# Selective scan issued between the tiles of the z, q, k and v projection, and two empty pieces of the expert loop left out

## The reference, cut to what matters

```
z, xbc, dt_f, dt_b, q, k, v, pin, gates = split(h @ w_in)          # h: modulated RMSNorm of x
ssd:   xbc = silu(conv5(xbc) + b);  xs (16 heads x 64), B, C (4 groups x 64)
       a = softplus(dt + bias) * -exp(a_log);  cs = cumsum(a) in each chunk of 128 tokens
       y[l] = sum_{s<=l} (C_l . B_s) exp(cs_l - cs_s) dt_s x_s  +  exp(cs_l) C_l . state      (forward and backward)
       y = rms_norm((y_f + y_b + d_skip * xs) * silu(z))
attn:  q, k normed, rotary on latent tokens, softmax over latent keys and cached context keys
pool:  windows 2, 4, 8, 16
merged = sum_i sigmoid(gate_i) * (branch_i @ w_i_out);  x += g1 * (merged @ w_out)
moe:   16 experts in 4 groups, the best group per token, top 2 in it:  x += g2 * moe(h2)
```

## Time and profile before

| what | value |
|---|---|
| median of the runs | 2563.08 us |
| profiled execution, its own time | 2565.21 us |
| its span on the core | 2563.4 us |
| PE busy, PE weight loads busy | 2225.8 us, 1924.2 us |
| DVE busy, ACT busy | 1517.6 us, 1128.6 us |
| mean granted clock | 0.936 |

### The profile page before, as it was taken

How to read it: one execution, slowest core, us unless ns; L and a number is a source line. 1 busy time by engine, 2 the same in 40 slices (tenths; PEclk the granted TensorE clock), 3 DMA queues, 4 the chain that set the end, 5 groups by cost and what they waited for, 6 DMA issues and landing times. The chain is left out here.

```text
span 2563.4 us, 29114 instructions
## 1 busy us (share of the span) xinstructions
PE 2225.8 (87%) x11340; PEld 1924.2 (75%) x11340; DVE 1517.6 (59%) x2064; ACT 1128.6 (44%) x1453; POOL 8.3 (0%) x12
## 2 busy tenths in 40 slices
PE   5859954599999999999799988993899999999993
PEld 3559943497777789999689988882877777777772
DVE  4857446522655444444454454544587978889784
ACT  4833322223244443333233343332366757667661
POOL 0000000000000000000000000000000000000000
PEclk9979976699999999999899999996899999999995
DMA  6924412144343345554245555640288989889881
GB/s 229 382 69 132 132 54 73 41 125 136 112 130 117 111 136 181 181 181 156 95 149 184 185 164 189 205 157 19 68 283 315 328 276 343 283 302 336 280 287 52
DMA packets 126856, 459.94 MB, mean 179 GB/s; under 512 B 15408, under 2 KB 17232, under 8 KB 126320
## 3 DMA queue, kind: packets, MB, share of 16 engines
q1 hardware_dynamic: 126704, 457.92, 53.1%
HBM read 453.88 MB, written 3.98 MB: 179 GB/s over the span
## 5 line engine op out<-in xcount | busy, mean ns | idle before, releaser
L159 DVE TENSOR_TENSOR wlo<-raw,whi 128x1024 fp32r<-128x1024 f32 x832 | 1005.9, 1223 | 761.5 <-ACT whi L153 748.8
L153 ACT ACTIVATE whi<-raw 128x1024 fp32r<-128x1024 f32 x832 | 870.7, 1058 | 845.5 <-PE bank L171 565.8
L169 PE MATMUL bank<-hhi,whi 128*128 128x384 f32 x1664 | 563.3, 339 | 44.0 <-PEq L891 17.5
L171 PE MATMUL bank<-hhi,wlo 128*128 128x384 f32 x1664 | 558.9, 336 | 0.0
L170 PE MATMUL bank<-hlo,whi 128*128 128x384 f32 x1664 | 558.3, 336 | 0.0
L169 PEld LDWEIGHTS bank<-hhi,whi 128*128 128x128 f32 x1664 | 314.4, 189 | 59.6 <-issue 38.6
L170 PEld LDWEIGHTS bank<-hlo,whi 128*128 128x128 f32 x1664 | 314.2, 189 | 1.6
L171 PEld LDWEIGHTS bank<-hhi,wlo 128*128 128x128 f32 x1664 | 313.9, 189 | 0.0
L1938 PE MATMUL bank<-whi,group_hi 128*128 128x512 f32 x512 | 203.3, 397 | 4.2 <-DVE wlo L159 3.1
L1940 PE MATMUL bank<-wlo,group_hi 128*128 128x512 f32 x512 | 201.2, 393 | 0.0
L1939 PE MATMUL bank<-whi,group_lo 128*128 128x512 f32 x512 | 200.5, 392 | 0.0
(11 more groups left out here) (322 smaller groups left out, 2501.5 us busy)
## 6 DMA issues: line engine op xcount, KB each, us to landing
raw<-in_dense SPq DMA_DIRECT2D x448, 512.0 KB, 3.7
raw<-in_moe SPq DMA_DIRECT2D x384, 512.0 KB, 4.9
cs_rows_bc<-cs_rows SPq DMA_DIRECT2D x8, 768.0 KB, 4.0
x_mix<-in_x SPq DMA_DIRECT2D x1, 3072.0 KB, 14.7
merged<-in_x SPq DMA_DIRECT2D x4, 768.0 KB, 6.7
out_y<-merged SPq DMA_DIRECT2D x4, 768.0 KB, 3.3
pool_w_sb<-in_pool_w SPq DMA_DIRECT2D x1, 1024.0 KB, 6.2
w_router_sb<-in_w_router SPq DMA_DIRECT2D x1, 1024.0 KB, 4.8
```

The costliest lines, as they stand in the source:

```text
L153: self.nc.scalar.activation(self.whi[:, n % W, :], self.raw[:, n % R, :], ACT.Copy).then_inc(self.hi_done, 1)
L159: self.nc.vector.tensor_tensor(self.wlo[:, n % W, :], self.raw[:, n % R, :], self.whi[:, n % W, :].bitcast(F32), ALU.subtract).then_inc(se ...
L169: self.nc.tensor.matmul(out, self.whi[:, s, c], xhi[:, k, :], start=(k == 0), stop=False)
L171: last = self.nc.tensor.matmul(out, self.wlo[:, s, c], xhi[:, k, :], start=False, stop=(k == blocks - 1))
```

## The change

- `ssd_in_phase` keeps only its 24 xbc tiles and now ends with the release of its semaphores and a barrier.
- `ssd_scan_phase`, `ada_settle_phase` and `attn_in_phase` go. In their place `z_qkv_phase` runs the 16 z tiles and the 24 q, k, v tiles as 40 slots, and a `Scan(Side)` object gives each engine a piece of the scan after each slot. Step n takes two slots: slot 11 + 2n (call it A) and slot 12 + 2n (call it B).
- In a step the two DVE instructions L853 and L856 become 12 ACT instructions of 128 x 128: Relu(cs_token - cs_row), with the token's value as the bias, followed by exp with scale -1.
- x is no longer kept by token: each step transposes its own 6 blocks on PE (`turn`), and DVE makes x*dt straight from PSUM in two instructions.
- The conditioning operands are placed at the top of SBUF from the start.
- In the experts, group 0 issues no scatter and the last group no gather; the semaphore counts follow.

```diff
-            N.tile0 += 24
-            N.sp_tiles(sp, 4, 4)
...
-def ssd_scan_phase(N):
...
+class Scan(Side):
+    FIRST, TAIL = 11, 28
...
+    def sp(self, sp):
...
+        for n, (g, d) in enumerate(self.steps):
+            if n >= 2:
+                for _ in range(2 if n > 2 else self.FIRST + 5 - 11):
+                    yield
+                sp.wait_ge(self.s_y, n - 1)
+            sp.dma_start(self.csb[:, n % 2]..., io.scratch[r0:r0 + 4, :]...).then_inc(self.s_csb[n % 2], 16)
...
+    def pe(self, pe):
...
+        for n, (g, d) in enumerate(self.steps):
+            pe.wait_ge(self.s_xdd, n + 1)
+            pe.wait_ge(self.s_stout, n)
+            ...                                        # states, two matmuls
+            yield
+            if n + 1 < len(self.steps):
+                turn(n + 1)                            # 6 transposes, and C.B where a group begins
+            pe.wait_ge(self.s_gated, 2 * g)
+            pe.wait_ge(self.s_m, n + 1)
+            ...                                        # outputs, 12 + 8 matmuls
+            last.then_inc(self.s_y, 1)
+            yield
...
+    def act(self, act):
...
+            act.wait_ge(self.s_csb[n % 2], 16 * (n // 2 + 1))
+            if n >= 2:
+                act.wait_ge(self.s_y, n - 1)
+            A(ec[rows, :, :], csb[rows, n % 2, :, T_CTX:T], ACT.Exp).then_inc(self.s_ec, 1)
+            act.wait_ge(self.s_wsub, n + 1)
+            A(self.wt[:, :, :], self.wt[:, :, :], ACT.Exp).then_inc(self.s_wexp, 1)
+            act.wait_ge(self.s_ec, n + 1)
+            for h in range(4):
+                for c in range(NCH):
+                    hc = 16 * d + 4 * g + h
+                    A(row[:, h, c * P:(c + 1) * P], row[:, h, c * P:(c + 1) * P], ACT.Relu, bias=cstok[:, c, hc:hc + 1],
+                      scale=-1.0).then_inc(self.s_d, 1)
+            act.wait_ge(self.s_d, 12 * (n + 1))
+            A(row, row, ACT.Exp, scale=-1.0).then_inc(self.s_dexp, 1)
+            yield
+            states(n)
+            yield
...
+def z_qkv_phase(N):
...
+            for s in range(slots):
+                if s % 2 == 0:
+                    pe.wait_ge(N.evac, N.blk0 + s // 2 + 1)
+                N.pe_tile(pe, 0, 0, s, N.bank[s // 2 % 2][:, 0:T], N.hhi, N.hlo, 8 * (s % 2), KB)
+                next(beside, None)
...
-def attn_in_phase(N):
...
-                            if t == SCATTER_AT[m]:
+                            if t == SCATTER_AT[m] and i + half:
                                 scatter(i, half, m)
...
+                            if i * 2 + half == NG - 1:
+                                break
                             if t == tiles[0]:
                                 pe.wait_ge(E.s_gl, picked(i, half) + p)
```

More of the change, by code:

```diff
@@ L187, in ada_phase @@
     csilu = N.keep("cond_silu", [P, KB, 2], F32)
[L188 to L193, removed]
+    cst = N.cst = N.keep_top("cond_parts", [P, KB, P], F32R)
+    bada = N.b_ada = N.keep_top("b_ada_sb", [P, 96], F32)
+    rows = N.ada_rows = N.keep_top("ada_rows", [P, 512], F32)
+    four = N.ada_four = N.keep_top("ada_four", [P, 4, 4], F32)
     sq = N.keep("x_squares", [P, 2, 4, T], F32)
@@ L884, in ada_settle_phase @@
[L884 to L898 removed]
+    N.tile0 += 24
@@ L1095, in __init__ @@
         self.sq = keep("head_squares", [P, 2, T], F32)
-        N.at = at = max(N.at, end)
+        N.at = max(N.at, end)
+        self.vt = keep("v_tok", [P, 4, 256], F32)
+        S["gate_at"], N.at = N.at, N.arena
+        at = N.at
         self.sel = keep("head_sel", [P, 10, 32], F32)
@@ L1806, in group @@
                             N.act_hi(act, i, body, half * GL + t)
-                        if t < 4:
+                        if t < 4 and i + half:
                             out_high(i, half, t)
@@ L1817, in group @@
                         for p, (bank, _tiles, at) in enumerate(PICKS):
-                            if t == at:
+                            if t == at and i * 2 + half < NG - 1:
                                 group_high(picked(i, half), p, bank, E.xhi[1 - half])
@@ L1956, in group @@
                             if t == ACT_TR[jj]:
-                                pe.wait_ge(E.s_x, scattered(i, half) * 2 + (2 * sum(at < t for at in SCATTER_AT) + 2))
+                                pe.wait_ge(E.s_x, scattered(i, half) * 2 + (2 * sum(at < t for at in SCATTER_AT if i + half) + 2))
                                 pe.wait_ge(E.s_act, i * 8 + ((g0 + half) * 4 + jj + 2))
@@ L1969, in group @@
                                 last.then_inc(E.s_ga, 1)
-                        if u == 0 and j > 0 and kind != "down":
+                        if u == 0 and j > 0 and kind != "down" and i * 2 + half < NG - 1:
                             pe.wait_ge(E.s_gl, picked(i, half) + sum(at < t for _b, _t, at in PICKS))
```

780 lines of the change are left out of this document (400 added, 380 removed).

## The result

| | before | changed |
|---|---|---|
| median of the runs | 2563.4 us (2561.8 to 2567.1, 4 runs) | 2429.8 us (2429.4 to 2431.3, 4 runs) |
| ratio, 95% interval | | 0.9478 (0.9461 to 0.9494) |
| profiled execution, own time / span | 2565.2 / 2563.4 us | 2430.0 / 2428.2 us |
| mean granted clock | 0.936 | 0.962 |

What follows compares the result with a forecast made beforehand. PE was taken as the bound, idle mainly in the scan; the woven phase, 240.7 us against 333.1, gives 92 us and the experts 21, so 113 off 2565.2 is 2452, less 2.1 for the median: 2450 us, range 2434 to 2485.

Steps and rivals of the forecast that it cites:

- step 3: Woven phase: the scan's own work on PE at full clock, 53.2 us together, of which outputs 26.2 and squares 6.
- step 6: Woven phase: PE's waits inside the scan, 6 us in all (chain for dt 2, first step 2.7, last 0.7); from above 22.
- the experts: Expert groups: first group without scatters, last without gathers; paces give 23 us less, taken as 21, bounds 6 and 28.
- convolution's tail and barrier (1): Before the first z tile: PE idle 7.1 us, 5.4 for the convolution's tail and 1.7 for the phase's end.
- tiles, clock, exit (2, 5): Woven phase: 40 tiles at 4.16 us, 166.4 us, plus 3.7 us for lowered clock and block exit.
- step 5: Woven phase's start and end: lowered clock after PE's idle time, with the block's exit, 3.7 us; from below 0.8.
- step 4: Woven phase: changing over between tile and scan on PE, 0.11 us a slot, 4.3 us for 40; bounds nothing and 13.
- U + 14.8: Scan step opening a group: U ends the tile before slot A; DVE's masked product comes 14.8 us later, PE needs it at 14.9.
- case C: Whole kernel: more gain, with no wait, changeover near zero and 28 us in the experts; 2434 us, chance 0.08.
- A: Scan step: bound by its engine-to-engine chain, 3 us longer, 24 us in all, 2474 us; chance 0.22, alone or with part of B.
- B: Experts: they stay bound by the DMA stream, so only some 7 us come back, 2464 us; chance 0.13.
- D: Woven phase: waits between tiles drop PE's clock to half, making the kernel slower than before, 2674 us; chance 0.03.

Runs made afterwards that it cites:

- the repeat: The changed kernel run once more with nothing altered, beside other kernels: 2429.9 us against 2560.8 for the kernel before, ratio 0.9493.
- experiment 5: Changed kernel with the decay differences moved back from ScalarE to VectorE (subtraction there, twelve Relu gone): 2436.7 us, ratio 0.9519.

## Why the prediction was right in kind and too small

The mechanisms held: the woven phase is PE's own work with few waits, and the experts follow their paces. What failed are three sizes, all on the cautious side: the outputs in step 3 (26.2 for 22.2 us), the waits in step 6 (6 for 2.8), and the experts (21 for 25 us of gain). A further 4 to 7 us came in code that no step names.

The forecast's sum for the woven phase, term by term, with what the traces and the run of the tiles alone gave:

| term (step) | forecast | measured |
|---|---|---|
| convolution's tail and barrier (1) | 7.1 | 6.5 |
| tiles, clock, exit (2, 5) | 166.4 + 3.7 | 169.2 |
| scan on PE, changeovers, waits (3, 4, 6) | 53.2 + 4.3 + 6 | 55.2 |
| sum | 240.7 | 230.9 |

1. *The tail and the barrier* were right: 6.5 us of idle time.
2. *Tiles* and *the clock* (step 5) were right: the clock read 0.93 over the first 23 us behind that idle time, and of the 3.7 us 2.8 were spent.
3. *The scan's own work* (step 3) has the term that failed most. The outputs: 2.14 + 1.14 us a step, 26.2 in all. From 342.59, where the first step's begin, to the next tile at 345.36 it is 2.77 us, 22.2 in all, 4.1 less. I had called the row of 2.14 us in the earlier trace rows one of full clock; a window over just that row reads 0.79, and the same twelve matmuls take 1.77 to 1.80 at 1.00. The squares took 5.3 for 6.
4. *Waits inside* (step 6): 2.8 for 6. The first step's 2.07 (forecast 2.7) and the last one's 0.74 (0.7) were as counted; the chain for dt cost nothing here and 0.2 in the repeat, where I had 2.
5. *Changeovers* (step 4). Outputs, squares and waits make 8.0 of the 63.5 - 55.2 = 8.3 us, so what is left of steps 3 and 4, 4.3 us of changeovers and the small pieces, was right together to 0.3 us. Each by itself wasn't measured, so errors in them may cancel.
6. *The step.* The chain that I followed gave the masked product at U + 14.8 against PE's 14.9. That count was for a step that opens a group, and the trace has it so: 0.15 to 0.3 us ahead in the three such steps behind the first. For the others I had 0.7 us or more, and they have 0.5 to 1.1. The loads on ScalarE and VectorE show the same two kinds of step from the other side. The wait for `cs_rows_bc` never showed, though the rows now take 6.0 us to land instead of 4.0.
7. *The experts.* Group 0: 8.2 for 9, the last group 17 for 14 (142.7 to 142.9 against 159.3 to 160.4 in four executions), 25 in all. The paces alone gave 23; I took off 2 for the stream, and that was wrong: at a DMA share of 0.94 and 0.95 the shortened stretches ran at 1.57 and 1.40 us a tile, under my 1.66 and 1.45.

Together: 102 and 25 make 127 us. The medians fell by 131 and 134 us in the two comparisons; the missing 4 to 7 are no step of mine. The traces have 3.5 and 6.0 us less in code that no edit touches, which is within the spread of one program there; how much of it the change itself gives is not shown. The range was too narrow for two reasons: its lower end was case C's sum (by its own terms 2450 - 6 - 4.3 - 7, so 2433 and not 2434) with nothing left for the error of the other terms, and nothing stood for an execution's draw, some 7 us wide (1171.4 to 1178.1) in the unchanged stretch alone.

The rivals: A needed a step dearer by 3 us than it was; B did not appear in any window; C was the nearest, with the outputs mis-sized besides; D's mechanism was seen for 1.6 to some 7 us a kernel, in the kernels with waits added and in one execution without. That the changed kernel's own traces show none of it behind the first step's wait is in part luck: one execution in seven with that wait paid 1.6 us. The Trainium skill, page "TensorE: Matmul & The Clock Gate", section "HAM oscillation — how this bites in real kernels", has a kernel whose matmuls come in bursts, with DMA waits of 3 to 5 us between them, start each burst at the slow clock. The runs bear it out only in part, and their waits are shorter: behind 2.07 us the clock stayed at 1.00 in six executions and fell to 0.50 in one, and within one execution it fell behind 2.18 us and stayed behind 2.20.

## What to carry to other kernels

Look first at weaving a chain of short dependent pieces between the tiles of an engine-bound stretch, and at shortening the chain after that: here the same pieces, and 24 more transposes, cost 55.2 us of PE instead of a stretch of 162.9, and with the differences left on VectorE (experiment 5) all but 7 us of the gain was there. Read the granted clock of every row that prices a term, since rows from an idle stretch make the woven form look dearer than it is. Behind such a weave the slack of the other engines differs from step to step (here 0.15 to 1.1 us in 14), and what overruns it can cost more than itself through the clock.

## What the runs showed of the hardware that I had not expected

- A wait of about 2 us on PE is enough for the granted clock to fall to 0.50, but it need not: behind a single wait of 2.07 or 2.08 us it stayed at 1.00 in six executions and fell in one (1.6 us lost); behind 2.18 us it fell and behind 2.20 us it stayed, in one execution. In three kernels with two waits in the first step, under 2 us apart (1.35 and 2.08, 1.45 and 2.08, 2.97 and 1.41 us), it fell each time, for some 6 us. What decides it stays open.
- A short phase behind a wait can take one of several lengths from execution to execution: 32 products with ones, behind a wait of 2.9 us, took 10.6, 12.0 or 13.6 us in one and the same stretch of code, at a granted clock of 1.00, 0.88 and 0.77.
- The same load of 768 KB (median of eight) landed in 3.8 to 4.1 us beside an almost idle DMA (share 0.13 in the old scan) and in 5.4 to 6.1 beside the tiles' stream (share 0.40 over the woven stretch of the changed kernel).
